# Attention scores of mixer A from float32r high and low parts, with a step's two heads from two key groups

## What is computed

```python
q = apply_axial_rope(rms_norm(q, q_g), cos, sin)      # 512 x 16 x 64
k = apply_axial_rope(rms_norm(k, k_g), cos, sin)      # 512 x 4 x 64
kc = rms_norm(pkv[..., :A_KV_WIDTH].reshape(b, lc, A_KV_HEADS, HEAD_DIM), k_g)
k_all = jnp.concatenate([kc, k], axis=1)              # 768 keys
def block(qi):                                        # 128 queries at a time
    s = jnp.einsum('bqkgd,bskd->bkgqs', qi, k_all).astype(jnp.float32) * ATTN_SCALE
    p = jax.nn.softmax(s, axis=-1).astype(v_all.dtype)
    return jnp.einsum('bkgqs,bskd->bqkgd', p, v_all)
yx = (o * jax.nn.silu(z)) @ w_out
sc = jnp.einsum('bqkgd,bskd->bkgqs', qc, kc).astype(jnp.float32) * ATTN_SCALE   # 256 context queries, context keys alone
x = x + g_x * yx
```

## Time and profile before

| | us |
|---|---|
| median of 3 runs | 1643.35 |
| lowest, highest | 1642.24, 1645.04 |
| the profiled execution | 1641.75 |
| its span | 1640.0 |
| PE, PEld busy | 1554.6 (95%), 1215.7 (74%) |
| DVE, ACT, POOL busy | 729.8 (44%), 621.5 (38%), 657.3 (40%) |
| chain that ended last | PE 83%, DVE 7%, ACT 3%, POOL 3%, issue 3%, DMA 1% |

### The profile page before, as it was taken

One profiled execution on the slowest core, in us unless ns is written; L12 is line 12 of the kernel. 1 busy time (PEld: TensorE's weight loads), 2 busy tenths in 40 slices (PEclk: granted clock), 3 DMA queues, 4 the chain that ended last, 5 costly groups with the idle time before them and its releaser, 6 DMA issues.

```text
span 1640.0 us, 25018 instructions
## 1 busy us (share of the span) xinstructions
PE 1554.6 (95%) x9858; PEld 1215.7 (74%) x9858; DVE 729.8 (44%) x1707; ACT 621.5 (38%) x1301; POOL 657.3 (40%) x640
## 2 busy tenths in 40 slices
PE   5998999999899999999998899999999999999997
PEld 3886777777588888787876687878878866655755
DVE  4434444455532534444355463543424454455033
ACT  3344444444432533333344353434322343333221
POOL 2534444433532533433335444435346344333252
PEclk8999999999999999999999899999999999999998
DMA  9110111110123222222221222312122222110221
GB/s 395 35 71 27 53 53 52 53 52 27 52 78 127 79 71 84 103 78 103 78 103 52 78 84 78 104 52 90 65 77 78 81 75 78 52 52 26 78 97 57
DMA packets 22148, 128.20 MB, mean 78 GB/s; under 512 B 2448, under 2 KB 2576, under 8 KB 8080
## 3 DMA queue, kind: packets, MB, share of 16 engines
q1 hardware_dynamic: 21888, 126.35, 21.4%
q10 hardware_dynamic: 144, 0.26, 0.1%
HBM read 124.50 MB, written 2.10 MB: 77 GB/s over the span
## 4 chain that ended last, share of the span: by engine, by line
PE 83%; DVE 7%; ACT 3%; POOL 3%; issue 3%; DMA 1%; SPq 0%; POOLq 0%; DVEq 0%; ACTq 0%
PE PS L1414 15%; PE PS L1416 14%; PE PS L1415 14%; PE PS L1494 7%; PE PS L1504 6%; PE PS L1529 6%; PE PS L1660 3%; PE PS L1409 3%; PE PS L1410 3%; PE PS L1411 3%; DVE sm L2108 2%; PE PS L1670 2%; PE PS L1582 1%; PE PS L1574 1%; PE PS L1427 1%
## 5 line engine op out<-in xcount | busy, mean ns | idle before, releaser
L2429 POOL TENSOR_TENSOR WL<-W,WH 128x512 fp32r<-128x512 f32 x280 | 367.3, 1327 | 320.9 <-ACT WH L1690 320.6
L1414 PE MATMUL PS<-HX,WH 128*128 128x512 f32 x1008 | 420.7, 417 | 10.6 <-DVE LX L2036 2.6
L1415 PE MATMUL PS<-LX,WH 128*128 128x512 f32 x1008 | 398.7, 395 | 0.0
L1416 PE MATMUL PS<-HX,WL 128*128 128x512 f32 x1008 | 398.2, 395 | 0.0
L1414 PEld LDWEIGHTS PS<-HX,WH 128*128 128x128 f32 x1008 | 192.8, 191 | 61.4 <-issue 16.7
L1416 PEld LDWEIGHTS PS<-HX,WL 128*128 128x128 f32 x1008 | 192.3, 191 | 42.6
L1415 PEld LDWEIGHTS PS<-LX,WH 128*128 128x128 f32 x1008 | 193.2, 192 | 36.8 <-issue 3.4
L1690 ACT CAST WH<-W 128x512 fp32r<-128x512 f32 x296 | 171.9, 617 | 46.9 <-DMA W<-in_wu 21.0
L2108 DVE TENSOR_REDUCE sm<-PS 128x1 f32<-128x512 f32 (+4 forms) x224 | 150.0, 670 | 69.2 <-PE PS L1494 64.5
L1776 ACT ACTIVATE AR<-PS,sm 128x768 f32<-128x768 f32 (+4 forms) x160 | 115.5, 722 | 171.6 <-DVE sm L2113 101.2
L2496 POOL TENSOR_SCALAR AR<-AR,sm 128x768 f32<-128x768 f32 (+1 forms) x96 | 75.9, 791 | 193.5 <-DVE sm L2124 193.5
(11 more groups left out here) (273 smaller groups left out, 2464.5 us busy)
## 6 DMA issues: line engine op xcount, KB each, us to landing
W<-in_wu SPq DMA_DIRECT2D x98, 1024.0 KB, 4.8
AR<-in_wu SPq DMA_DIRECT2D x8, 1024.0 KB, 11.6
AR<-in_biasb SPq DMA_DIRECT2D x32, 256.0 KB, 2.6
XX<-in_xt SPq DMA_DIRECT2D x2, 1024.0 KB, 6.4
out<-XX SPq DMA_DIRECT2D x8, 256.0 KB, 2.2
XC<-in_xt SPq DMA_DIRECT2D x1, 1024.0 KB, 14.6
C<-in_cc SPq DMA_DIRECT2D x1, 770.5 KB, 8.8
CS<-in_cs SPq DMA_DIRECT2D x1, 512.0 KB, 10.5
```

The source lines that it names most:

```text
L1414: e.matmul(o, wh, xh, start=(k == 0), stop=False)
L1415: e.matmul(o, wh, xl, start=False, stop=False)
L1416: t = e.matmul(o, wl, xh, start=False, stop=(k == 7))
L2429: e.tensor_tensor(WL[:, d, a:z], W[:, n % 2, a:z], WH[:, d, a:z].bitcast(F32), ALU.subtract).then_inc(*s_wl_pool.by(n, q))
```

## The change

The keys are no longer doubled. They are split into a high part kH (ACT, one copy of 128 x 768 per m instead of four of 64 x 768) and a low part kL (DVE, `a_key_low`), in the arena where kd lay. So partitions 0 to 63 of kH[m] hold key group 2m and 64 to 127 hold 2m+1, and a pair now has one head from each: the host reorders the columns of the query and gate weights and the rows of the output weights (`heads_a`). Each finished query is split into qH (ACT, `a_query_high`) and qL (DVE, `a_query_low`). These lie over columns 1024 to 4095 of XX (blocks 2 to 7 of x), and x is loaded a second time into them after score 41 and score 47 (`x_again`); the residual of `aout` waits for it. `score` makes three float32r products in place of one float32 product. The fill of pair p no longer waits for the output of pair p-2: only its gate projection waits, and only for a score that is further back. The numbering of semaphores for the keys is shared out anew, without other waits.

```diff
+        kH, kL = [ar.parts(NT) for _ in range(2)], [ar.parts(NT) for _ in range(2)]
-        kd = ar(4 * NT).rearrange("p (c n) -> p c n", c=4)
+        qH, qL = [[XXp[:, 1024 + 1536 * i + NT * j:1024 + 1536 * i + NT * (j + 1)] for i in range(2)] for j in range(2)]
...
-                    need = [(s_kd, (m,)) for m in range(2)] + [(s_qrope, (pair,))]
+                    need = [(s_kd, (i,)) for i in range(2)] + [(s_kl, (i,)) for i in range(2)] + [(s_qh, (pair,)), (s_ql, (pair,))]
...
+            if n in (41, 47):
+                do("x_again", n // 47)
...
             for pair in range(1, 8):
-                yield from until(lambda: pair < 2 or pair - 2 in done_a)
                 yield from query_group(pair, 0, FX, {2: ride_mm, 6: ride_tr})
                 yield PAUSE
                 yield from query_group(pair, 1, FC)
                 yield PAUSE
-                yield from gate_group(pair, 0, FX, {2: lambda: query_sums(pair, FC), 3: lambda: query_turn(pair, FC), 6: lambda: query_rope(pair)})
+                yield from until(lambda: pair < 2 or 6 * pair - 7 in scored_a)
+                yield from gate_group(pair, 0, FX, {2: lambda: query_sums(pair, FC), 3: lambda: query_turn(pair, FC), 5: lambda: query_rope(pair), 7: lambda: query_high(pair)})
                 yield PAUSE
-                yield from gate_group(pair, 1, FC, {3: ride_mm_x, 6: ride_tr} if pair == 7 else {})
+                yield from gate_group(pair, 1, FC, {1: lambda: query_low(pair), **({3: ride_mm_x, 6: ride_tr} if pair == 7 else {})})
...
         query_rope(0)
-        run(gate_group(0, 1, vr))
+        query_high(0)
+        run(gate_group(0, 1, vr, {3: lambda: query_low(0)}))
...
+                    if name == "a":
+                        for x, y in ((0, 0), (1, 0), (0, 1)):
+                            for h in range(2):
+                                a, b, l, r = s.qk[h][i]
+                                t = e.matmul(PS[:, s.score[h] + a:s.score[h] + b], l[x], r[y], start=(x + y == 0), stop=(y == 1))
...
             def a_key_rope(m):
                 w.wait_ge(*s_krope(m))
-                for kv in (0, 1):
-                    for po in (0, 64):
-                        t = e.copy(kd[po:po + 64, 2 * m + kv, :], krr[m][64 * kv:64 * kv + 64, :])
-                t.then_inc(*s_kd.by(m))
+                e.copy(kH[m], krr[m]).then_inc(*s_kd.by(m))
+            def a_query_high(pair):
+                w.wait_ge(*s_qrope(pair))
+                w.wait_ge(*(s_score("a", 6 * pair - 7, 1) if pair >= 2 else s_scaled(0, 7)))
+                e.copy(qH[pair % 2], qT[pair % 2]).then_inc(*s_qh.by(pair))
+            def a_key_low(m):
+                w.wait_ge(*s_kd(m))
+                e.tensor_tensor(kL[m], krr[m], kH[m].bitcast(F32), ALU.subtract).then_inc(*s_kl.by(m))
-                await_all(w, [(s_score, ("a", 6 * pair - 7, 1))] if pair >= 2 else H_A)
+                await_all(w, [(s_ql, (pair - 2,))] if pair >= 2 else H_A)
+            def a_query_low(pair):
+                w.wait_ge(*s_qh(pair))
+                e.tensor_tensor(qL[pair % 2], qT[pair % 2], qH[pair % 2].bitcast(F32), ALU.subtract).then_inc(*s_ql.by(pair))
+                if name == "aout" and j == 0 and m > 1:
+                    w.wait_ge(*s_again[m // 5](m // 5))
+            def x_again(i):
+                w.wait_ge(*s_score("a", (41, 47)[i], 1))
+                a, b = 1024 + 1536 * i, 2560 + 1536 * i
+                e.dma_start(XX[:, a:b], xt[:, a:b]).then_inc(*s_again[i].by(i))
```

More of the change, by code:

```diff
@@ L185, in build, with twin @@
         WH, WL = sb("WH", [P, 2, 2048], F32R), sb("WL", [P, 2, 2048], F32R)
-        XX, XC = sb("XX", [P, KC * T]), sb("XC", [P, KC * LC])
+        def twin(name, shape):
+            with nc.sbuf_tensor(name, shape, F32) as full:
+                pass
+            return full, sb(name + "_parts", shape, F32R)
+        XX, XXp = twin("XX", [P, KC * T])
+        XC = sb("XC", [P, KC * LC])
         HX, HC = sb("HX", [P, KC * T], F32R), sb("HC", [P, KC * LC], F32R)
@@ L192, in build @@
         sm = sb("sm", [P, 640])
[L193 removed]
+        AR, ARp = twin("AR", [P, ASZ])
         class Rows:
@@ L254, in build @@
         s_r2, s_fgg = signal("norm2"), signal("norm2_gain")
-        s_ksq, s_kraw, s_ksum, s_kvar, s_krs, s_kb, s_kn = (signal("key_" + n) for n in ("squares", "raw", "sums", "var", "rs", "broad", "normed"))
-        s_krot, s_ksin, s_kcos, s_krope, s_kd = (signal("key_" + n) for n in ("rotated", "sin", "cos", "roped", "placed"))
+        s_ksum, s_kb, s_krot = shared("keys_pe", 3)
+        s_ksq, s_kd = shared("keys_act", 2)
+        s_kraw, s_kvar, s_kn, s_ksin, s_krope, s_kl = shared("keys_dve", 6)
+        s_krs, s_kcos = shared("keys_pool", 2)
+        s_qh, s_ql = signal("query_high"), signal("query_low")
+        s_again = [signal(f"x_again{i}", 16) for i in range(2)]
         s_av = signal("values_a")
@@ L743, in query_rope, with query_high, query_low @@
             do("a_query_rope", pair)
+        def query_high(pair):
+            do("a_query_high", pair)
+        def query_low(pair):
+            do("a_query_low", pair)
             ready_q.add(pair)
@@ L836, in build @@
         values((3,))
+        key_work[3]()
         query_sums(0, vr)
@@ L843, in build @@
         query_rope(0)
-        run(gate_group(0, 1, vr))
-        attention("a", [s for pair in range(8) for s in steps_a(pair)], SA, TA, PbA, PTbA, OA, fill_a(), (8 * 14 * (T + LC) + 14 * T) / 100 + 5 * 3, posted_a)
+        query_high(0)
+        run(gate_group(0, 1, vr, {3: lambda: query_low(0)}))
+        attention("a", [s for pair in range(8) for s in steps_a(pair)], SA, TA, PbA, PTbA, OA, fill_a(), (8 * 14 * (T + LC) + 14 * T) / 100 + 5 * 3, posted_a, scored_a.add)
         do("a_last_gate")
@@ L2676, in cols @@
         return w.reshape(8, P, N // 256, 256).transpose(2, 1, 0, 3).reshape(N // 256, P, 2048)
+    heads_a = np.array([64 * (8 * (p // 4) + p % 4 + 4 * h) for p in range(8) for h in range(2)])
+    heads_a = (heads_a[:, None] + np.arange(64)).reshape(-1)
     w2 = a["w_in_2"][0]
```

33 lines of the change are left out of this document (20 added, 13 removed).

## The result

The changed kernel takes 1639.26 us (median of 9 runs, 1636.82 to 1641.82), beside 1643.41 us of the kernel before (9 runs, 1641.03 to 1646.86): ratio 0.997, 95% interval 0.9957 to 0.9983. Faster, by 4.2 us; the forecast was 1628, 15.2 us under the execution profiled before. The profiled spans are 1635.7 and 1640.0 us.

The account below looks back on a forecast made before the run. PE (TensorE), with 83% of the chain of waits, was taken to bound the kernel. Terms -8.8, -8.1, -3.1, +0.9, +0.9, +2 and +1 sum to -15.2 us from 1641.75: 1626.6, as a median 1628; range 1618 to 1640.

Parts of the forecast that it names:

- scores: Attention A's scores: three float32r products, heads side by side, shorten 32 full and 16 short steps: -8.8 us.
- fill: Attention A, scores 6 to 37: the new fill condition removes waits for exponentials: -8.1 us, bounds -9.3 and -5.
- third place: Pairs 2 to 5: the query's last add falls into the rotation's step, 0.5 us each: +2 us, bounds 0 and 5.
- clock: Behind steps 6 and 7: the half-clock stretch at 158.50 returns to full clock: -3.1 us, bounds -3.1 and 0.
- score 0: At score 0: the gate now stands behind ACT's high and DVE's low part: +0.9 us, bounds 0 and 2.
- score 42: Before score 42: high and low part come behind the query's last add: +0.9 us, bounds 0.3 and 2.
- end: End of attention A: a gate wait goes, modulation row, step 43 and output splits cost: +1 us, bounds -1 and +4.
- behind score 47: After attention A's last score: second loads of x cost nothing, up to 4 us once if a weight load were late.
- rivals A: Scores: the two heads take turns in float32r, +30.8 us in place of -8.8, about 1667 us; chance 0.09.
- rival B: Scores: weight loads of second and third term wait for the matmul on their rows, +21 us, 1649 us; chance 0.04.
- rival D: Attention A: the scores' gain goes to waits for exponentials; fill and half the clock gain stay, 1637 us; chance 0.13.

Follow-up runs that it names:

- scores alone: Changed kernel with the old fill condition back at its old place; 1657.55 us, ratio 1.007.
- one term: Changed kernel computing only high times high of the three score products, all splits kept; 1626.03 us, ratio 0.9881.
- power last: Changed kernel with POOL's power of the query's norm moved behind the cosine product; 1632.53 us, ratio 0.9917.
- add, high and low part later: Changed kernel with the query's last add, high part and low part behind the gate's first half in pairs 1 to 6; 1633.0 us, ratio 0.9923.
- high part behind the gate: Changed kernel with only the query's high part moved behind the gate in pairs 1 to 6; 1633.63 us, ratio 0.9933.
- the fill alone: Kernel before with only the new fill condition, scores still one float32 product, no query split; 1635.93 us, ratio 0.9938.

## Why the prediction was right in part, step by step

The terms beside what the two profiles show:

| | forecast | measured |
|---|---|---|
| scores: TensorE's other time, score 0 to 47 | -8.8 | -7.0 |
| fill: idle time up to score 41, without the third place | -8.1 | -7.8 |
| clock, score 0 to 47 | -3.1 | +3.0 |
| score 0 (measured: all of the time before it) | +0.9 | -0.7 |
| score 42 | +0.9 | +1.9 |
| third place | +2 | +7.5 |
| end: idle time, score 41 to 47, without score 42 | +1 | -3.1 |
| behind score 47 | 0 | +1.9 |
| sum | -15.2 | -4.3 |

(Differences are taken before rounding.)

**Scores: right.** Twelve records in 1.32 us, 1.25 to the next group, six in 0.62 and 0.56 (1.26 and 0.56 forecast); rivals A and B fall. The float32r pairs of 64 rows do run side by side, and the loads of the later terms cost nothing: all twelve fall within 1.12 us of the 1.25. That is against the rule of the Trainium skill that rival B took (TensorE: Matmul & The Clock Gate, Part 3, "What overlaps and what doesn't").

**Fill: right.** The waits for exponentials at steps 6, 7, 13, 19, 25 and 31, 8.1 us together, are gone; the one at 37 is 0.82 of 1.17. Alone the new condition takes 8.4 us of waits before full steps' scores (12.3 to 3.9), for a forecast of 8.1, and with the clock's 3.1 it brings score 41 10.2 us sooner.

**Clock: right in its place, wrong as a sum.** The stretch at 158.5 went. One at 147.3 and two behind score 42 came; -3.1 was forecast and +3.0 measured; with the next it is the largest miss. The one at 147.3 begins 1.4 us behind pair 1's stall of 2.81 us, and such a stretch stands there in both other kernels with a stall of 2.8 us or more (scores alone, one term), and in none where it is 1.4 or less (power last; add, high and low part later; high part behind the gate).

**Third place of the new steps: the step that failed.** It said that the add in the rotation's step would cost 0.5 us in each of pairs 2 to 5, because a weight split was missing from POOL's queue, and that the high part in front of the exponential did no harm since its maximum was as late. The measured cost is 6.4 us more of idle time before transposes up to score 41 (3.2 to 9.6), and 1.1 more before an output product: 7.5 for +2, over the bound of 5. Of the stalls themselves, 5.8 stand in pairs 2 to 5, for which the 2 was meant, and 1.6 more than before in pair 1, for which nothing was put down. Two links weren't seen. The high part stands in front of the gate's tanh too, and DVE's half of the gate in front of the next maximum and the output's product (shown by moving the high part alone: 0.49 and less are left of 1.57 and 1.62, with the add as late and as long as before). And the add grows to 1.32 us beside POOL's scaling, as the 1.80 of the earlier trace rows had allowed; I had drawn on that row for the low part only. Its share in the stalls no run shows by itself.

**Score 0: right**, 1.94 in place of 1.08, though the score itself comes 0.7 us sooner. **Score 42: mis-sized**, 2.12 in place of 0.23: +1.9 for +0.9, inside its bounds of 0.3 to 2. The sum left out the tanh and the gate (0.59 + 0.69) between high and low part.

**End of the attention: right in its time by luck.** Score 42 and the end were to cost +1.9 together, and from score 41 to 47 the profile is 1.9 longer. But idle time was to rise by 1.9, score 42 included, and fell by 1.2, so that without score 42 it fell by 3.1, beyond the bound of -1; TensorE's other time fell by 1.2 with the shorter scores; and 4.3 were lost to the clock, which no term had.

**What the sum missed otherwise.** TensorE's time outside idle and slow stretches fell by 5.9 us between scores 0 and 41, where the scores' own shortening is 28 x 0.24 + 13 x 0.08 = 7.8. The difference lies with the fill: it alone raises this time by 1.6 (285.5 to 287.1), and from there to the changed kernel it falls by 7.5. Why the fill raises it stays open; if half of the busy time is more than a slow stretch really costs, it would look like this, since before has such a stretch there and the fill alone has none. The same comparison shows where the scores' gain went: from the fill alone to the changed kernel, up to score 41, TensorE's other time falls by 7.5 us and its idle time rises by 8.0 (4.8 to 12.8), with 1.7 more lost to the clock. In this, and in the run with one term, rival D has a part of the truth: the scores' gain is handed to waits, of DVE and ACT queues and not of exponentials. That its 1637 is the nearest of the forecasts to 1639 is in part luck: by its own terms (no 8.8, and half of the 3.1) it comes to 1638, and its waits, those for exponentials, didn't come.

Behind score 47, where nothing was changed but the second loads of x, the profile is 1.9 us longer, 1.2 of it idle time and 0.7 clock. This part takes 1181.5 to 1188.2 us in the thirteen profiles, with 14.7 to 23.5 lost to the clock, so 1.9 can't be told from no change; and totals of single profiles can differ by that much for nothing that was changed.

Two things stay open further: why the clock falls behind one of two equal waits, and how much of the 5.3 us between the changed kernel and the fill alone (0.997 and 0.9938) is the clock's: in their profiles 6.0 us are lost to it between scores 0 and 47, and none.

## What to carry to other kernels

A copy or cast put into an in-order queue costs what stands behind it, not its own length: follow each new operation to the next one that the bottleneck engine awaits, across both engines, and past every hand-over between them. Measure each half of a change that has two; here one line of the fill's condition was worth more than the whole, and the three terms paid, 2.5 to 3.7 us of the 8.8 expected, only after the power was moved behind the product that others wait for. A faster matmul in a loop gives its full time only in steps where no other queue is within that time of being late.

## What the runs showed of the hardware

Two float32r matmuls on 64 rows each, on different halves of the array, run side by side like float32 ones: a full step of 3 x (512 + 256) columns for two heads in 1.25 us. The weight loads of all three terms fall into this time. A DVE operation with two SBUF operands grows beside a wide POOL operation that began first (0.68 to 1.32, 0.95 to 1.95); where DVE began first, POOL's grows (0.48 to 1.11 for a scaling of 256 columns). A POOL operation on 12 columns that began first costs the add beside it nothing, though it lasts 2.28 us. And the granted clock is half for 3.4 to 6.8 us behind some idle stretches of 1.6 to 3.1 us and not behind others of the same length (1.9 us at one place: a half-clock stretch in two kernels, none in five), with 1.5 to 3.4 us of TensorE's work lost in each: a change of a few tenths of a per cent can be as much the clock's as its own.
